# Rotary query parts copied first and read from PSUM, and latent scores computed ahead of a weight split, a convolution and the value copies

## The reference

```python
qh = (_rms_norm(c_q, mla_q_norm_g) @ mla_w_uq).reshape(b, s, MLA_HEADS, MLA_NOPE + MLA_ROPE)
q_nope, q_rope = qh[..., :MLA_NOPE], _rope(qh[..., MLA_NOPE:], pos)
kv = (_rms_norm(c_kv, mla_kv_norm_g) @ mla_w_ukv).reshape(b, s, MLA_HEADS, MLA_NOPE + MLA_V)
k_nope, v_mla = kv[..., :MLA_NOPE], kv[..., MLA_NOPE:]
k_rope = _rope(k_r[:, :, None, :], pos)[:, :, 0, :]
y_mla = _mla_attention(q_nope, q_rope, k_nope, k_rope, v_mla)   # 4 heads, softmax, causal
qk_c = silu(_causal_dwconv(concat([mq, mk]), mlstm_conv_w, mlstm_conv_b))
# _rope: x1, x2 = halves; [x1 * cos - x2 * sin, x2 * cos + x1 * sin]
```

## Time and profile before

| | |
|---|---|
| time, median of 3 runs | 1296.04 us (1295.96 to 1297.54) |
| the profiled execution: its own time | 1297.05 us |
| its span in the trace | 1294.8 us |
| TensorE busy | 1280.5 us (99%) |
| VectorE busy | 890.7 us (69%) |
| ScalarE busy | 638.3 us (49%) |
| DMA, mean over the span | 181 GB/s |

### The profile page before, as it was taken

The page is one execution under the profiler, slowest core; times in us unless marked ns, Lnnn a source line. Parts: engine busy times, 40 slices in busy tenths (PEclk is TensorE's granted clock), DMA queues, the critical chain, the costliest instruction groups (busy, mean ns, idle before and its releaser), DMA issues.

```text
span 1294.8 us, 18576 instructions
## 1 busy us (share of the span) xinstructions
PE 1280.5 (99%) x7985; PEld 1150.2 (89%) x7985; DVE 890.7 (69%) x1086; ACT 638.3 (49%) x654; POOL 71.2 (5%) x59
## 2 busy tenths in 40 slices
PE   8999999999999999999999999999999999999998
PEld 7888889998999988888888888899989998888886
DVE  6666667998675676665675666779976766766655
ACT  5444446684644444444454444456745443544441
POOL 0399000000000000000000000000000000000000
PEclk9999999999999999999999999999999999999999
DMA  8755547643566555555556655466436565655562
GB/s 295 234 187 188 193 147 223 185 130 102 193 194 196 171 181 180 186 193 195 173 185 195 195 190 190 140 196 196 131 99 199 191 196 163 192 187 188 187 192 95
DMA packets 176401, 234.80 MB, mean 181 GB/s; under 512 B 8064, under 2 KB 146944, under 8 KB 176192
## 3 DMA queue, kind: packets, MB, share of 16 engines
q1 hardware_dynamic: 175936, 231.78, 56.0%
q0 software_dynamic: 240, 1.71, 0.4%
q10 hardware_dynamic: 144, 0.13, 0.1%
HBM read 232.56 MB, written 1.05 MB: 180 GB/s over the span
## 4 chain that ended last, share of the span: by engine, by line
PE 97%; DVE 1%; DMA 1%; ACT 1%; issue 0%; DVEq 0%
PE ps L1477 22%; PE ps L1452 21%; PE ps L1460 11%; PE ps L1380 11%; PE ps L1379 11%; PE ps L1378 11%; PE ps L1443 5%; PE ps L1400 1%; PE ps L1412 1%; DMA raw<-w_in 1%; PE ps L1662 1%; PE ps L1621 0%; PE ps L1622 0%; ACT rot_sw L633 0%; PE ps L1648 0%; PE ps L1649 0%
## 5 line engine op out<-in xcount | busy, mean ns | idle before, releaser
L838 DVE TENSOR_TENSOR wlo<-raw,whi 128x2048 fp32r<-128x2048 f32 (+1 forms) x218 | 492.5, 2277 | 205.3 <-ACT whi L547 205.0
L547 ACT ACTIVATE whi<-raw 128x2048 fp32r<-128x2048 f32 (+1 forms) x218 | 413.3, 1898 | 282.9 <-DMA raw<-w_in 112.2
L1452 PE MATMUL ps<-xpair,whi 128*128 128x512 f32 x1216 | 290.0, 390 | 0.0
L1452 PEld LDWEIGHTS ps<-xpair,whi 128*128 128x128 f32 x1216 | 225.7, 188 | 45.3
L1378 PE MATMUL ps<-xpair,whi 128*128 128x256 f32 x800 | 224.1, 280 | 0.0
L1380 PE MATMUL ps<-xpair,wlo 128*128 128x256 f32 x800 | 222.5, 278 | 0.0
L1379 PE MATMUL ps<-xpair,whi 128*128 128x256 f32 x800 | 222.4, 278 | 0.0
L1460 PEld LDWEIGHTS ps<-xpair,wlo 128*128 128x128 f32 x1216 | 154.5, 189 | 6.1
L1460 PE MATMUL ps<-xpair,wlo 128*128 128x256 f32 x1216 | 156.4, 281 | 0.0
L1379 PEld LDWEIGHTS ps<-xpair,whi 128*128 128x128 f32 x800 | 150.5, 188 | 0.4
L1378 PEld LDWEIGHTS ps<-xpair,whi 128*128 128x128 f32 x800 | 150.1, 188 | 0.4
(11 more groups left out here) (234 smaller groups left out, 1598.7 us busy)
## 6 DMA issues: line engine op xcount, KB each, us to landing
raw<-w_in SPq DMA_DIRECT2D x60, 1024.0 KB, 5.2
raw<-ffn_w_down SPq DMA_DIRECT2D x44, 1024.0 KB, 4.9
raw<-ffn_w_gate SPq DMA_DIRECT2D x40, 1024.0 KB, 5.4
raw<-ffn_w_up SPq DMA_DIRECT2D x40, 1024.0 KB, 5.4
raw<-w_br SPq DMA_DIRECT2D x12, 1024.0 KB, 5.1
raw<-w_out SPq DMA_DIRECT2D x8, 1024.0 KB, 4.8
raw<-ffn_w_gate SPq DMA_DIRECT2D x6, 512.0 KB, 3.8
raw<-ffn_w_up SPq DMA_DIRECT2D x6, 512.0 KB, 4.7
```

The lines of the kernel that those rows point to most:

```text
L547: act.activation(unit(whi, n), unit(raw, n), ACT.Copy).then_inc(w_hi, 1)
L838: dve.tensor_tensor(w_low(n), unit(raw, n), unit(whi, n).bitcast(F32), ALU.subtract).then_inc(w_lo, 1)
L1452: pe.matmul(ps[:, bank, :], wh[:, kk, cols], xpair[:, kk, :, :], start=kk == 0, stop=kk == KC - 1, skip_group_check=True)
```

## The change

Within the latent attention of each mixer:

1. ScalarE no longer makes the straight copy `rot` of the rotary query parts (the retention parts keep theirs). VectorE's first rotary product reads them from their PSUM bank. The four exchanged copies now stand ahead of the copy of `qn1`, and the two key copies ahead of `hi(13)`.
2. ScalarE runs `exps(0)` and `exps(1)` right behind `hi(13)`, ahead of `hi(14)` and the first Silu.
3. VectorE no longer runs `conv(2)` between `lo(11)` and `lo(12)`; it stands behind `lo(14)`. `scores(0)` and `scores(1)` follow the rotation directly, then `lo(13)`, `probs(0)`, `probs(1)`, the two value copies, `row_t`, `lo(14)`, `conv(2)`, `conv(3)`.
4. The values `v0`, `v1` go to banks 3 and 0 and the transposes `T0`, `T1` to banks 4 and 5; TensorE's waits follow, so that the value products no longer wait for the query copies, and `mla_values(0)` waits for the value copies.

```diff
+    BANK |= {"v0": 3, "v1": 0, "T0": 4, "T1": 5}
...
             def swap(job, half):
 
-                copy(rot[:, :], job)
+                if half == ROPE:
+                    copy(rot[:, :], job)
...
-            copy(flat(q_nope[:, 2:4, :]), "qn1").then_inc(q_copied, 1)
             act.wait_ge(rotated, l * 6 + 1)
             swap("qr", 32).then_inc(rot_copied, 1)
-            hi(m0 + 13)
+            copy(flat(q_nope[:, 2:4, :]), "qn1").then_inc(q_copied, 1)
             act.wait_ge(k_done, l + 1)
             copy(flat(k_nope[:, 0:2, :]), "kn0").then_inc(k_copied, 1)
             copy(flat(k_nope[:, 2:4, :]), "kn1").then_inc(k_copied, 1)
+            hi(m0 + 13)
+            exps(0)
+            exps(1)
             hi(m0 + 14)
...
-                dve.tensor_tensor(wide(rot), wide(rot), factors[0], ALU.mult)
+                dve.tensor_tensor(wide(rot), halves(ps[:, BANK["qr"], :]) if dst is None else wide(rot), factors[0],
+                                  ALU.mult)
...
-            conv(2)
             lo(m0 + 12)
             rotate(1, None, cos_m, sin_m)
+            scores(0)
+            scores(1)
             lo(m0 + 13)
+            probs(0)
+            probs(1)
             dve.wait_ge(w_used, done_no(m0 + 11))
             for t in range(TT):
                 dve.tensor_copy(v_mla[:, t, :], ps[:, BANK[f"v{t}"], :]).then_inc(v_copied, 1)
-            scores(0)
-            scores(1)
...
-            probs(0)
-            probs(1)
             lo(m0 + 14)
+            conv(2)
             conv(3)
...
-            for t in (1, 0):
-                if t == 0:
-                    pe.wait_ge(rot_copied, l * 6 + 2)
-                else:
-                    pe.wait_ge(q_copied, l * 2 + 2)
+            pe.wait_ge(lat_std, l + 1)
+            for t in range(TT):
...
-            pe.wait_ge(lat_std, l + 1)
+            pe.wait_ge(q_copied, l * 2 + 2)
             mla_turn(1)
...
+            pe.wait_ge(v_copied, l * 6 + 4)
             mla_values(0)
```

More of the change, by code:

```diff
@@ L722, in mixer @@
             act.activation(ml_qk[:, 0:4, :], ml_qk[:, 0:4, :], ACT.Silu).then_inc(qk_silu, 1)
-            exps(0)
-            exps(1)
             hi(m0 + 15)
@@ L1785, in mixer @@
             mla_scores(3)
-            pe.wait_ge(v_copied, l * 6 + 3)
             project(14, "rk0")
@@ L1801, in mixer @@
             spread(0)
-            pe.wait_ge(v_copied, l * 6 + 4)
             project(15, "rk1")
```

## The result

| | before | after |
|---|---|---|
| time, median (range) of 6 runs each | 1296.79 us (1294.59 to 1299.46) | 1305.43 us (1304.02 to 1308.16) |
| ratio to before, 95% interval | | 1.0070 [1.0058, 1.0082] |
| the profiled execution, and its span | 1297.05 us, 1294.8 | 1305.22 us, 1302.9 |

The change makes the kernel slower by 8.6 us. The forecast was 1302.1, with a range that ended at 1304.5: the direction was right, and the loss was 2.5 us larger than what was summed up.

What follows compares the result with a forecast made beforehand. TensorE bounds the kernel, busy 1280.5 of 1294.8 us, with VectorE level. VectorE's lag of 3.15 less 0.1 to spare gives 3.05 per layer, 6.1 over two; 1296.04 + 6.1 = 1302.1 us, range 1299.0 to 1304.5.

Steps and rivals of the forecast that it cites:

- The rotation earlier: At the first latent scores, the wait for q_rope goes and TensorE is 1.05 us earlier per layer.
- The source in PSUM: VectorE's rotary product reading PSUM costs nothing more, bounds 0 to 0.02 us; the skill's figures would give 0.06 more.
- VectorE's idle time: New VectorE waits of 2.7 us before the rotation and 1.6 at the scores make it 3.1 to 3.2 late.
- ScalarE: It waits 1.2 and 0.4 us for maxima; TensorE waits 0.9 for pt at the value product, swallowed by the later wait.
- Rival C: The 0.9 us wait before the value product is not swallowed: loss 3.95 per layer, 1303.9 us; chance 0.05.
- What TensorE pays at `mla_turn(2)`: VectorE's lag of 3.15 less 0.67 to spare starts mla_turn(2) 2.5 us later, out of a wait of about 2.6.
- rival D: Clock halves behind the new 2.6 us wait, costing 3 us more per layer: 1308 us; chance 0.04.
- At unit 16 TensorE needs the `rk0` copies: With 0.1 us to spare at most, TensorE waits another half microsecond there and is 3.05 us late per layer.
- Rivals A: VectorE reaches mla_turn(2) no later than now: 2.1 us faster, 1293.9, chance 0.04; or no change, chance 0.05.
- B: Half the lag, 1.6 us, as scores finish sooner or VectorE wins back time before probs(2): 1299.0 us; chance 0.08.
- TensorE never makes up for a loss: Beyond unit 16, spare time is some microseconds, and TensorE's 3.05 us loss per layer stays to the end.

Runs made afterwards that it cites:

- e3: The changed kernel with conv(2) put back between lo(11) and lo(12) on VectorE: 1297.72 us, ratio 1.0009 to the kernel before.
- e5: The changed kernel with ScalarE's first Silu moved behind the pt copies: 1309.04 us, ratio 1.0098 to the kernel before.
- e1: The changed kernel with 16 extra matmuls, result unused, on TensorE ahead of its wait at mla_turn(2): 1300.62 us, ratio 1.0028 to the kernel before.
- e6: The kernel before with one extra VectorE reduction of 1056 columns behind lo(15), a measured lag of 1.15 us: 1297.35 us, ratio 1.0009.
- e7: The kernel before with two extra VectorE reductions behind lo(15) and 16 extra TensorE matmuls ahead of mla_turn(2): 1300.09 us, ratio 1.0037.
- e2: The kernel before with two extra VectorE reductions of 1416 columns behind lo(15), result unused: 1305.64 us, ratio 1.0072.
- e8: The changed kernel with VectorE's old order put back, ScalarE keeping its new order: ratio 1.0056 to the kernel before.
- e9: The changed kernel with ScalarE's old order of exponentials and first Silu put back, VectorE keeping its new order: ratio 1.0081 to the kernel before.

## Why the prediction was wrong

The waits were forecast rightly. The sum was short of one term, the half clock, which stood among the rivals and was put at nothing in the sum, and it had one term of 1.1 us that does not exist.

1. *The rotation earlier*, 1.05 us: measured 1.1 (the shift at the scores). The wait for `q_rope` is gone.
2. *The source in PSUM*, nothing: 0.69 us against 0.69, as the two rows said. The 0.06 us more that the prediction worked out from the Trainium skill (VectorE: DVE Perf Modes) does not show.
3. *VectorE's idle time*, 2.7 and 1.6, lag 3.1 to 3.2: measured 2.70, 1.67, and 3.15 more idle time, of which 0.19 was made up by shorter busy time, so that the lag is 2.97. `e3` shows that `conv(2)` was what filled the larger gap.
4. *ScalarE*, waits of 1.2 and 0.4, `pt` ready at 273.2, TensorE waiting 0.9: measured 1.23, 0.32, 273.37, and 0.56 and 0.74. Nested in the later wait, as put (`e5`). Rival C is out.
5. *What TensorE pays at `mla_turn(2)`*, 3.15 - 0.67 = 2.5 us: measured 2.5 in both layers. In part this is luck: the lag is 2.97 and the spare time 0.52, so both terms were about 0.15 too large, and the errors cancel. The wait itself is 2.2 and 2.4 instead of 2.6.

Two steps failed. The smaller: "At unit 16 TensorE needs the `rk0` copies", for 0.55 us per layer, 1.1 in all. Its wait counts copies, and I counted one too far, and took the banks of `rq0` and `rq1` for those of `rk0` and `rk1`; the two times lay 0.1 us apart in the earlier trace rows by chance. `e1` and `e6` show that nothing is there. Without it the sum is 5.0 us, a ratio of 1.0039; `e1`, the changed kernel with its clock kept up, has 1.0028 [1.0018, 1.0039]. As this error made the forecast too high, it hid part of the other.

The larger: step 5 let the work behind the wait of 2.6 us run at full clock, and half clock was only rival D, at a chance of 0.04. D said 3 us per layer and 1308; the trace has 3.0 and 1.6. The steps of the trace add up to 2 x 2.45 + 4.6 = 9.5 us, and its end shows 8.1, because of the 0.7 between the mixers and the 0.9 behind the second; the medians differ by 8.6. `e1` and `e7` show it from the runs, at 5.4 and 4.5 us. The error was in the weighing: the only rows I had were a longest idle time of 1.75 us without a fall and a fall behind the last matmul, and a wait of 2.6 lay between them. That is an open case, and I gave it the chance of a remote one. With D at a third, or a range to 1308, the forecast would have said what the rows bear. The rule that the prediction named (the Trainium skill, TensorE: Matmul & The Clock Gate, Part 1: half the clock is the idle state, activity releases it) agrees with the direction: 16 idle-time matmuls keep the clock at 1.00.

Rivals A and B are out: between `conv(3)` and `probs(2)` no more than the 0.2 us of shorter busy time was won back. "TensorE never makes up for a loss" was right only roughly: 0.7 us came back between the mixers.

## What to carry over

Where a bound engine meets a chain of another engine with little to spare, add up the other engine's idle time before and after a reordering: a dependent chain moved forward exposes its waits, and what used to fill them (`conv(2)` here) is what has to stay. Price a new TensorE wait of two microseconds or more not at its length alone but also with half clock behind it, here from nothing to 3.0 us behind a wait of 2.2 to 2.4. That one such wait of a kernel was seen at full clock is no assurance for the next: `e2` has one of each kind. And before two close times are called a dependence, count what the semaphore counts.

## What the runs showed of the hardware

The fall of the clock does not follow from the wait's length alone. Waits of 2.2 to 2.4 us were followed by 6.8 us (changed kernel, layer 1), 3.4 us (its layer 2, and layer 2 of `e2`) or nothing (layer 1 of `e2`) at half clock. All those of 2.7 and 2.9 us (`e8`), 3.2 to 3.4 (`e5`) and 3.9 (`e9`) brought some. The fall came when TensorE was at work again in the changed kernel (at 285.8, the wait having ended at 285.2), and while it was idle in layer 1 of `e9` (at 283.5) and of `e5` (at 284.0), though not in layer 2 of either (at 932.0 and 929.2, the waits having ended at 931.3 and 928.9). Where it comes late, the work that pays for it is what stands behind the wait, the weight unit above all. What decides between the cases at equal length stays open. It is not the order of the program: the two layers of `e2` have the same waits in the same places (0.9 us for `q_rope`, then 2.4), one without a fall and one with it, and its executions differ among themselves.

Sixteen matmuls put into a wait of 2.2 to 2.4 us, about 1.9 us of work, kept the clock at its upper level in every run of two kernels (`e1` and `e7`, mean granted clocks of 0.998 to 1.000).
